# Layer-0 input projection of a two-layer decoder trunk by one level of Strassen's scheme, with block sums on GpSimd

## The reference, cut to what matters

```
xn = rmsnorm(h, pre_g[0])                            # 512 x 1024
proj = xn @ w_in                                     # 1024 x 7168
a_b, a_c, a_x, a_gate, b_u, b_v, b_gate = split(proj) # 1024 columns each
y_a = a_b * causal_short_conv(a_c * a_x, conv_w) * silu(a_gate)
v = layernorm(b_v, ln_g, ln_b)      # 4 chunks of 128 tokens, 8 groups of 128 channels
s = einsum('gts,bnsgc->bntgc', tril(w_s), v) + b_s
y_b = b_u * s * silu(b_gate)
y = concat(y_a, y_b) @ w_out
h = h + rmsnorm(y, post_g[0])
h = h + sigmoid(rmsnorm(h, ple_g[0]) @ w_ple_gate[0]) * (p[0] @ w_ple[0])
```

## Time and profile before

| | us |
|---|---|
| device time, median of 3 runs | 1057.43 |
| lowest and highest of the runs | 1055.49, 1058.51 |
| the profiled execution: span from the first to the last instruction | 1055.9 |
| PE busy in it | 1033.2 |
| DVE busy in it | 505.8 |
| ACT busy in it | 325.0 |
| POOL busy in it | 57.3 |

### The profile page before, as it was taken

How to read it: one execution, slowest core, us unless ns; L and a number is a source line. 1 busy time by engine, 2 the same in 40 slices (tenths; PEclk the granted TensorE clock), 3 DMA queues, 4 the chain that set the end, 5 groups by cost and what they waited for, 6 DMA issues and landing times.

```text
span 1055.9 us, 12689 instructions
## 1 busy us (share of the span) xinstructions
PE 1033.2 (98%) x4702; PEld 854.6 (81%) x4702; DVE 505.8 (48%) x748; ACT 325.0 (31%) x556; POOL 57.3 (5%) x107
## 2 busy tenths in 40 slices
PE   6999999999999999998999999999999999999998
PEld 4888888888888888787888888888888888888876
DVE  5244454447664224656554453543355235441735
ACT  5221212122112124544332322332233222322622
POOL 2010000000000002203000000000000000000400
PEclk9999999999999999999999999999999999999999
DMA  7322232322322422221322222123222222143122
GB/s 299 120 92 108 80 120 79 116 82 80 104 95 70 180 109 80 80 95 65 120 80 81 80 80 108 55 81 112 82 79 79 79 80 80 40 180 120 41 80 79
DMA packets 17107, 102.22 MB, mean 97 GB/s; under 512 B 2096, under 2 KB 3120, under 8 KB 5936
## 3 DMA queue, kind: packets, MB, share of 16 engines
q1 hardware_dynamic: 17072, 101.74, 26.5%
HBM read 99.64 MB, written 2.10 MB: 96 GB/s over the span
## 4 chain that ended last, share of the span: by engine, by line
PE 93%; DVE 2%; POOL 2%; ACT 2%; issue 1%; DMA 1%; POOLq 0%; SPq 0%; DVEq 0%; ACTq 0%
PE bank L1174 17%; PE bank L1172 17%; PE bank L1173 17%; PE bank L1186 12%; PE bank L1188 12%; PE bank L1187 12%; PE bank L1415 1%; ACT square L464 1%; PE bank L1406 1%; PE bank L1418 1%; PE bank L1393 1%; POOL rstds L386 1%; PE bank L1263 1%; PE bank L1354 1%; POOL rstds L385 1%
## 5 line engine op out<-in xcount | busy, mean ns | idle before, releaser
L741 DVE TENSOR_TENSOR w_lo<-raw,w_hi 128x1024 fp32r<-128x1024 f32 x174 | 206.3, 1227 | 468.1 <-ACT w_hi L453 468.0
L453 ACT ACTIVATE w_hi<-raw 128x1024 fp32r<-128x1024 f32 x174 | 174.8, 1053 | 568.5 <-PE bank L1174 327.1
L1172 PE MATMUL bank<-x_hi,w_hi 128*128 128x512 f32 x776 | 305.2, 393 | 0.0
L1174 PE MATMUL bank<-x_hi,w_lo 128*128 128x512 f32 x776 | 302.3, 390 | 0.0
L1173 PE MATMUL bank<-x_lo,w_hi 128*128 128x512 f32 x776 | 302.2, 389 | 0.0
L1174 PEld LDWEIGHTS bank<-x_hi,w_lo 128*128 128x128 f32 x776 | 145.6, 188 | 30.5
L1173 PEld LDWEIGHTS bank<-x_lo,w_hi 128*128 128x128 f32 x776 | 145.7, 188 | 30.1
L1172 PEld LDWEIGHTS bank<-x_hi,w_hi 128*128 128x128 f32 x776 | 145.7, 188 | 29.7
L1186 PE MATMUL bank<-w_hi,x_hi 128*128 128x512 f32 x320 | 128.1, 400 | 0.6 <-DVE w_lo L741 0.5
L1187 PE MATMUL bank<-w_lo,x_hi 128*128 128x512 f32 x320 | 125.9, 393 | 0.0
L1188 PE MATMUL bank<-w_hi,x_lo 128*128 128x512 f32 x320 | 125.8, 393 | 0.0
(11 more groups left out here) (145 smaller groups left out, 755.5 us busy)
## 6 DMA issues: line engine op xcount, KB each, us to landing
raw<-in_slots SPq DMA_DIRECT2D x87, 1024.0 KB, 4.8
...
```

What stands on the lines that cost most here:

```text
L453: act.activation(w_hi[:, r, c], raw[:, r, c], ACT.Copy).then_inc(hi_ready, 1)
L741: dve.tensor_tensor(w_lo[:, r, c], raw[:, r, c], w_hi[:, r, c].bitcast(F32), ALU.subtract).then_inc(lo_ready, 1)
L1172: pe.matmul(bank[b][:, :], w[0][:, k, at], x_hi[:, k], start=(k == 0), stop=False)
L1174: done = pe.matmul(bank[b][:, :], w[1][:, k, at], x_hi[:, k], start=False, stop=(k == KD - 1))
```

## The change

The projection is computed by one level of Strassen's scheme in the variant with seven block products and shared sums. The left matrix (512 x 1024) is cut in four blocks of 256 x 512; the weights are taken 1024 columns at a time, a *unit*, cut in four blocks of 512 x 512, of 1 MB each. There are 7 units: one of b_v columns ("v"), four of a_c, a_x, a_gate, a_b ("a"), two of b_gate, b_u ("b"). A unit has seven products of a left block and a weight block, each of 2 x 4 x 3 = 24 matmuls, where the eight plain block products would have 8 x 24.

- The left operands, seven blocks with high and low parts, are made once at the start. Four are blocks of the transposed input, and three are sums, made by DVE from copies that ACT takes (`f11`, `f21`, `f12`, `f5`).
- Four of the seven weight blocks of a unit are sums. POOL makes each with one `tensor_tensor` of 128 x 2048 in the raw buffers `raw7` (5 of them): `sums_of`, 28 in all.
- ACT rounds each of the seven blocks (`hi7`) and DVE takes the rest (`lo7`), two halves each, in a ring of three.
- The products are added up in PSUM where they can be. What is left is copied by ACT (`b_copy`, `s5_copy`) and subtracted by DVE (`c_make`, `s5_make`, each two instructions of 128 x 512 for a unit).
- All results are token-major. Gate and product of the A heads are made in that form (`z_make`, `g_make`, with 256 columns), transposed by PE (`conv_transposes`, 8 calls with 8 transposes), and then go through the convolution. The B heads are mixed by 8 float32 matmuls of 512 columns (`mix`) and transposed after it (`mix_transposes`, 8 calls with 4 transposes).
- The scale and offset of the layer norm go from DVE to POOL, 16 instructions of 128 x 512 in units 2, 3 and 4 (`ln_affine`).
- Two float32 matmuls on data without use are put between the first transposes (`warm`).
- The place of `h` in SBUF is used for other tiles in the projection, and `h` is loaded again ahead of the tail. The tail and layer 1 keep their instructions; their loads and tiles have other places. Loops of the layer-0 projection are written out.

The core of the diff, with what the prediction speaks of:

```
+UNITS = 7
+ORDER_FIRST = (1, 2, 5, 6, 3, 7, 4)
+ORDER = (1, 5, 6, 2, 3, 7, 4)
+L_PLACE = {1: 0, 5: 1, 6: 2, 2: 3, 3: 4, 7: 5, 4: 6}
+RING = 3
+ROWS_IN = 4 * UNITS
+KIND = "vaaaabb"
+STEPS = [(u, p) for u in range(UNITS) for p in (ORDER if u else ORDER_FIRST)]
+STEP = {what: g for g, what in enumerate(STEPS)}
+BX, BV, BA, BY, BZ = range(5)
+SOURCE = {1: BX, 5: BA, 6: BX, 2: BZ, 3: BY, 7: BV, 4: BA}
+SUMS = {5: 1, 6: 2, 7: 3, 4: 4}
...
+    raw7, = region(R_AT, ("raw7", [P, 5, SLOT], F32))
+    l_hi, l_lo = region(L_AT, ("l_hi", [P, 7, 4, 2 * P], F32R), ("l_lo", [P, 7, 4, 2 * P], F32R))
...
+        def block_in(u, b):
+            row_of = {BX: 0, BV: 1, BZ: 2, BY: 3}
+            sp.dma_start(raw7[:, b], slots[4 * u + row_of[b]]).then_inc(b_in[b], 16)
...
+        block_in(0, BZ)
+        block_in(0, BV)
+        block_in(0, BY)
...
+        sp.wait_ge(first_scaled, TILES)
+        sp.wait_ge(warm, 1)
+        row(ln_g, ln_rows[0:1, :], ln_in)
+        row(ln_b, ln_rows[1:2, :], ln_in)
+        for u in range(UNITS):
+            sp.wait_ge(sum_done, sum_at(u, 4))
+            sp.wait_ge(w7_lo_ready, split_done(u, 6))
+            if u + 1 < UNITS:
+                block_in(u + 1, BX)
+            sp.wait_ge(w7_lo_ready, split_done(u, 2))
+            if u + 1 < UNITS:
+                block_in(u + 1, BZ)
+            sp.wait_ge(w7_lo_ready, split_done(u, 3))
+            if u + 1 < UNITS:
+                block_in(u + 1, BY)
+            else:
+                load(0, 0, wait=False)
+                load(1, 1, wait=False)
+            sp.wait_ge(w7_lo_ready, split_done(u, 7))
+            if u + 1 < UNITS:
+                block_in(u + 1, BV)
...
+        def add(u, p, dst, one, two):
+            if p == 5:
+                pool.wait_ge(b_in[BX], 16 * (u + 1))
+                pool.wait_ge(b_in[BV], 16 * (u + 1))
+                if u:
+                    pool.wait_ge(w7_lo_ready, split_done(u - 1, 4))
+            if p == 6:
+                pool.wait_ge(sum_done, sum_at(u, 5))
+                pool.wait_ge(b_in[BY], 16 * (u + 1))
+                pool.wait_ge(w7_lo_ready, split_done(u, 1))
+            if p == 4:
+                pool.wait_ge(sum_done, sum_at(u, 6))
+                pool.wait_ge(b_in[BZ], 16 * (u + 1))
+                pool.wait_ge(w7_lo_ready, split_done(u, 5))
+            pool.tensor_tensor(raw7[:, dst], raw7[:, one], raw7[:, two], ALU.add).then_inc(sum_done, 1)
+        def sums_of(u):
+            add(u, 5, BA, BX, BV)
+            add(u, 6, BX, BA, BY)
+            add(u, 7, BV, BV, BY)
+            add(u, 4, BA, BX, BZ)
...
+        sums_of(0)
+        pool.wait_ge(const_in, 16 * 6)
         pool.affine_select(out=wt[:, :, :], in_=wt[:, :, :], compare_op=ALU.is_ge, fill=0.0, base=0,
                            pattern=[[0, 8], [1, P]], channel_multiplier=-1).then_inc(wt_ready, 1)
+        sums_of(1)
...
+        def ln_affine(g):
+            def over_tiles(row):
+                return row[:, g * P:(g + 1) * P].rearrange("p (a c) -> p a c", a=1).to_broadcast([P, TILES, P])
+            if g == 0:
+                pool.wait_ge(ln_in, 32)
+                pool.wait_ge(vst_ready, TILES)
+            link(pool.tensor_tensor(v_even[:, g], v_even[:, g], over_tiles(ln_g), ALU.mult))
+            pool.tensor_tensor(v_even[:, g], v_even[:, g], over_tiles(ln_b), ALU.add).then_inc(ln_done, 1)
+        sums_of(2)
+        for g in range(3):
+            ln_affine(g)
+        sums_of(3)
+        for g in range(3, 6):
+            ln_affine(g)
+        sums_of(4)
+        for g in range(6, 8):
+            ln_affine(g)
+        sums_of(5)
+        sums_of(6)
...
+        def hi7(g):
+            u, p = STEPS[g]
+            if p in SUMS:
+                act.wait_ge(sum_done, sum_at(u, p))
+            else:
+                act.wait_ge(b_in[SOURCE[p]], 16 * (u + 1))
+            if g >= RING:
+                act.wait_ge(prod_done, 2 * (g - RING) + 2)
+            for half in range(2):
+                c = slice(half * SLOT // 2, (half + 1) * SLOT // 2)
+                act.activation(w7_hi[:, g % RING, c], raw7[:, SOURCE[p], c], ACT.Copy).then_inc(w7_hi_ready, 1)
...
+        def lo7(g):
+            if g >= RING:
+                dve.wait_ge(prod_done, 2 * (g - RING) + 2)
+            for half in range(2):
+                c = slice(half * SLOT // 2, (half + 1) * SLOT // 2)
+                dve.wait_ge(w7_hi_ready, 2 * g + half + 1)
+                dve.tensor_tensor(w7_lo[:, g % RING, c], raw7[:, SOURCE[STEPS[g][1]], c],
+                                  w7_hi[:, g % RING, c].bitcast(F32), ALU.subtract).then_inc(w7_lo_ready, 1)
...
+        for k in range(7):
+            if k == 0:
+                left_sum(5, f5)
+                dve.wait_ge(full_ready[11], 2)
+                dve.wait_ge(full_ready[5], 2)
+                dve.tensor_tensor(f21[:, :, :], f11[:, :, :], f21[:, :, :], ALU.subtract).then_inc(full_ready[7], 1)
+                dve.wait_ge(full_ready[7], 1)
+                dve.tensor_tensor(f11[:, :, :], f5[:, :, :], f11[:, :, :], ALU.subtract).then_inc(full_ready[6], 1)
+                dve.wait_ge(full_ready[6], 1)
+                dve.wait_ge(full_ready[12], 2)
+                dve.tensor_tensor(f12[:, :, :], f11[:, :, :], f12[:, :, :], ALU.add).then_inc(full_ready[3], 1)
+                left_sum(6, f11)
+                left_sum(3, f12)
+            if k == 4:
+                c_make(0, 1)
+            if k == 6:
+                s5_make(0, 1)
+            lo7(k + 2)
+            if k == 0:
+                left_sum(7, f21)
...
+        for u in range(1, UNITS):
+            was, now = KIND[u - 1], KIND[u]
+            for k in range(7):
+                g = 7 * u + k
+                if k == 0 and was == "a":
+                    for tp in range(2):
+                        g_make(u - 1, s5[:, tp], tp, 2 + tp, s5_free)
+                if k == 3:
+                    for tp in range(2):
+                        c_make(u, tp)
+                if k == 6:
+                    s5_make(u, 1)
+                if g + 2 < 7 * UNITS:
+                    lo7(g + 2)
+                else:
+                    lo(k - 5)
+                if k == 0:
+                    for tp in range(2):
+                        if was == "v":
+                            stats(0, 2 + tp, b_free, tp + 1)
+                            stats(1, 2 + tp, s5_made, tp + 1)
+                        elif was == "a":
+                            z_make(u - 1, b_of, tp, 2 + tp, b_free)
+                        else:
+                            wide_silu(u - 1, b_of, tp, 2 + tp, b_free)
+                            gu_make(u - 1, s5[:, tp], tp, 2 + tp, b_free, s5_free)
...
+                if k == 4:
+                    for tp in range(2):
+                        if now == "a":
+                            z_make(u, a_of, tp, tp, a_free)
+                        else:
+                            wide_silu(u, a_of, tp, tp, a_free)
+                if was == "a" and k in (2, 4):
+                    conv(2 * (u - 2) + (k - 2) // 2)
...
+                if k == 5:
+                    s5_make(u, 0)
...
+        def product(u, p, tp):
+            g = STEP[u, p]
+            r = g % RING
...
+            if p in (2, 6):
+                pe.wait_ge(b_copied, 2 * u + tp + 1)
+            if p in (3, 7):
+                pe.wait_ge(c_made, 2 * u + tp + 1)
+            if p == 4:
+                pe.wait_ge(s5_made, 2 * u + tp + 1)
+            dst = {1: a_of, 2: a_of, 5: c_of, 3: c_of, 6: b_of, 7: b_of, 4: b_of}[p](tp)
+            first = p in (1, 5)
+            tt = slice(tp * P, (tp + 1) * P)
+            for k in range(4):
+                if tp == 0 and k % 2 == 0:
+                    pe.wait_ge(w7_lo_ready, 2 * g + k // 2 + 1)
+                c = slice(k * SEQ, (k + 1) * SEQ)
+                left_hi, left_lo = l_hi[:, L_PLACE[p], k, tt], l_lo[:, L_PLACE[p], k, tt]
+                pe.matmul(dst[:, :], left_hi, w7_hi[:, r, c], start=(first and k == 0), stop=False,
+                          skip_group_check=True)
+                pe.matmul(dst[:, :], left_hi, w7_lo[:, r, c], start=False, stop=False, skip_group_check=True)
+                done = pe.matmul(dst[:, :], left_lo, w7_hi[:, r, c], start=False, stop=(k == 3),
+                                 skip_group_check=True)
+            done.then_inc(prod_done, 1)
...
+        def conv_transposes(n):
+            f = n % 2
+            v = n // 2 + 1
+            pe.wait_ge(a_free, 2 * v + 2)
+            pe.wait_ge(b_free, 2 * v + 2)
+            if n:
+                pe.wait_ge(conv_ready, n)
+            for t in range(TILES):
+                done = pe.transpose(bank[6][:, t * P:(t + 1) * P], z_tok[:, t, f * P:(f + 1) * P], ident[:, :])
+            done.then_inc(zt_ready, 1)
+            pe.wait_ge(c_free, 2 * v + 2)
+            pe.wait_ge(s5_free, s5_used(v, 1))
...
+        first_transpose(0)
+        for tp in range(2):
```

(19 more changed lines are left out.)

880 lines of the change are left out of this document (552 added, 328 removed).

## The result

The changed kernel takes 1116.76 us (1115.93 to 1117.09, four runs) against 1057.29: a ratio of 1.0568, 95% interval [1.0553, 1.0583]. It is 59 us slower, 25 more than forecast, and outside the range of 1040 to 1112. Its profiled execution has a span of 1114.3 us.

A forecast was written before the change was run, and what follows sets the result against it. PE was taken to bound the kernel. Span 1055.9 - 27.3 (PE's work) + 22.6 (unit 0) + 39.6 (later units) = 1090.8; with 1.5 for the median, 1092 us. Range 1040 to 1112; the forecast's own, 1072 to 1110.

The forecast's parts named there:

- PE's own work, -27.3 us: Projection on PE: 168 fewer matmuls take 38.1 us off, added float32 transposes and late first matmuls cost 10.8.
- DVE and POOL shut each other out: Shared SBUF ports: during a 4.0 us POOL sum no DVE instruction with two SBUF inputs starts, and the reverse.
- The rival of no exclusion: POOL's sums run beside DVE; only DVE's queue at the start is late, by 6.3 us: 1036 us, chance 0.16.
- PSUM operands pass: DVE's `c_make`, `s5_make` and `z_make`, reading PSUM and SBUF, are not held by POOL; otherwise up to 4 us more a unit.
- The sum of 4.0 us and the norm instruction of 1.1 us: Assumed POOL durations: 4.0 us for each of 28 sums, 1.1 us for each of 16 norm instructions.
- The bounds of 2.0 and 5.7: Limits in us for one POOL sum: 2.0 at the one-input rate, 5.7 with two reads and a write in turn.
- What POOL time is worth: Share of added POOL sum time on the path: half of 48 us for longer sums; 0.5 us a sum costs some 8.
- Unit 0, 22.6 us of waiting: First projection unit: PE waits on DVE work queued among POOL's sums, ending at 77.7 us in place of 55.1.
- The later units, 39.6 us: Units 1 to 6: PE waits mainly for `s5_make` and, at unit turns, `z_make`, delayed by sums and norm instructions; 39.6 us.
- The 1.1 us at P6 of unit 1: Part of unit 1's 6.0 us of waits: PE waits 1.1 us at product P6, besides 4.7 for `s5_make`.
- The clock: PE's clock falls in waits of 4 to 8 us, costing 2 us per ten matmuls; shares the longer-sums rival's 0.07.
- The rival of longer sums: Sums of 5.7 us, or PE's clock falling: 48 us more POOL time, half on the path; 1116 us, chance 0.07.

## Why the prediction was wrong

The direction and the mechanism were right. The time lies 25 us over the forecast. The step that failed is the price of POOL's work: how long its instructions last, and how much of that time counts. The steps in their order:

- **PE's own work, -27.3 us.** Right to about 3 us, on the good side. The kernel without sums has a span of 1031.6 us, with some 7.8 us of waits and slow matmuls in its projection, where before had 2.2. So PE's work is 1031.6 - 7.8 + 2.2 - 1055.9 = -29.9. Where the 3 us lie is not shown; the kernel before differs by as much from run to run. The mixing was priced rightly (see the last section).
- **DVE and POOL shut each other out.** Right, and shown: 75 of the 82 us that the sums cost go with their reading. The rival of no exclusion had 1036; the kernel in which POOL is busy as long and DVE is not held measured 1041.28.
- **PSUM operands pass.** Right: L1087 and L1096 took 0.68 us inside a sum, as the Trainium skill's "SBUF — State Buffer", section "Who interferes with whom", says of one SBUF input.
- **The sum of 4.0 us and the norm instruction of 1.1 us.** This is the first half of the failed step. They measured 4.63 and 1.47 (L544; L545 is 1.35). The bounds of 2.0 and 5.7 held the value; I took a value between, next to two inputs read in turn (3.9), with only one-input selects to go by. Giving POOL my own sizes took 18 to 20 of the 25 us off. The figure that I had set aside, 4.5 us in the Trainium skill's "GPSIMD Engine Reference", section 3.1, was the nearer: here 4547 ns least and 4630 median.
- **What POOL time is worth.** This is the second half. For longer sums I let half of their time count and said 8 us for half a microsecond a sum. The runs show 18.1 us for 20.0 of POOL's time, 15.7 of sums and 4.3 of norm: nine tenths (19.8 us by the ratios). Over all of the sums half is about right: their 137 us cost 75 by their reading. So the last microseconds of POOL cost more than the average one.
- **Unit 0, 22.6 us of waiting.** Some 23: 3.6, 12.1, 2.3, 0.5, 1.5 and 3.5 us. The second product did not start at 27.5 with ACT's copy done but at 38.70; the wait only moved up from the third product, as the run with an early `b_copy` showed. The 3.5 us ahead of P4 (76.61) I had not foreseen. Unit 0 ended at 82.2 us, where I had 77.7; the rest of this difference is slow cadence.
- **The later units, 39.6 us.** The waits for `s5` and `z_tok` came at the places foretold: 3.9, 10.4, 10.3, 9.4, 6.9 and 3.0 in units 1 to 6, against 6.0, 10.1, 10.1, 7.9, 3.5 and 2. Together 44 us, 4 more, and some 4 us in small waits that I had not. The 1.1 us at P6 of unit 1 did not come.
- **The clock.** I had it as a rival at 0.07, with a price of 2 us each time. It does fall, to 0.85 in the stretch shown above, and costs 17 us of PE time, but most of that replaces waits: the runs leave it 3 to 5 us.

The rival of longer sums had 1116, and 1116.76 was measured. That is luck: it asked for sums of 5.7 us and they last 4.63, and it let half of the added time count.

In the trace of the changed kernel the miss of 25 us is 10 us of waits beyond the 62 of the forecast, 15 us of slow cadence beyond the kernel before, 1 us less of other work, and 1 us more between span and median. What the clock alone is worth stays open between 3 and 5 us.

No version beats the kernel before while it computes the same: the best, the sums on DVE in a good order, is 0.25% slower. Its 28 sums of 2.28 us leave DVE busy for nine tenths of a unit, and PE's gain of some 30 us goes back as 26 us of waits, 16 of them in the first and the last unit, and 5 of slow cadence.
